# A hybrid decoder step: V, keys and keys' Gram of the recurrence on the opposite half of the array, and another order of VectorE's turn

## The chip, the cores and the metric

The kernel runs on one core of a Trainium2 chip. The metric is device time in microseconds of one execution: before the change the median of three runs is 1163.49 us (1162.94 to 1168.54).

## The reference, cut to what matters

One inference step of a decoder layer for 1024 prompt rows and 8 x 8 sample rows: a combined input projection, a convolution group and an RWKV-7 group side by side, an output projection, and a mixture of experts. The change touches the RWKV-7 recurrence alone, which runs for 8 heads of 64 channels:

```
def wkv_step(S, inp):
    r_t, w_t, k_t, v_t, kk_t, a_t = inp
    sa = einsum('bhvk,bhk->bhv', S, -kk_t)
    S = (S * w_t[:, :, None, :] + sa[..., None] * (kk_t * a_t)[:, :, None, :]
         + v_t[..., None] * k_t[:, :, None, :])
    y = einsum('bhvk,bhk->bhv', S, r_t)
    return S, y
```

Around it stand the token shift, the decay and the in-context learning rate from small projections, a norm of the keys per head, a group norm of y, a bonus term and an output gate.

## The kernel before, in words

The recurrence is computed in chunks of 64 tokens. Two chunks, 128 tokens, are one turn: turns j = 0 to 7 are the prompt, turn 8 the 64 sample rows. Two heads share the 128 partitions (channels p = 0 to 63 and 64 to 127), and there are four such pairs (CT = 4, index hp). Nearly every product of the recurrence is thus eight 64 x 64 matmuls, four on the array tile with rows and columns 0 to 63, four on the tile with rows and columns 64 to 127, taken in turn (`heads`, L1647).

Each engine has its own written-out program, in order, and they meet by semaphores. In turn j, with i = j - 1:

- TensorE (loop at L1791) forms the Gram of the b keys of turn j (`gram`, L1665: products within a chunk of all tokens' keys with all scaled a and r), the decay and learning rate of turn j + 1, the tokens of V (`to_tokens`, L1656: a transpose by a matmul with the identity), then for turn i the first product of level 4 (`level_y`), the first chunk's right-hand side (`chain_rhs`), the rest of level 4 (`level_x`), tokens of B, the Gram of the k keys of turn j, level 5's first product, tokens of K, the key norms of turn j + 1, the rest of level 5, y of turn i - 2 to channels, and then the chain for each of the two chunks: U (`chain_u`), the new state (`chain_s`), y (`chain_y`), the next right-hand side; between them bonus, cumulation of the decay for turn j + 1, and the gate of turn j - 3.
- Levels 4 and 5 combine inverses of 16 x 16 blocks to the inverse of a unit triangular 64 x 64 matrix. The inverses of the small blocks are made by VectorE on 64 partitions, one block each: SP moves the diagonal blocks to `u_blocks` in DRAM and back (L584, L587), VectorE works on `small_blocks` (L2425) and `whole_blocks` (L2434), ACT turns the result (`blocks_turned`, L1054), SP moves it by `x_blocks` (L592, L597) into XX, and TensorE's level 4 of the next turn waits for it (`inv_in`).
- VectorE (loop at L2513): masks the b Gram (`first_level`, L2394), adds the decay (`decay_add`, L2264), masks level 4 (L2416), the rest of the b Gram (L2402), centres the group norm, applies the conv norm, masks the k Gram (`masked_k`, L2408), masks level 5, small blocks, whole blocks, first new state (`new_state`, L2453 and L2456), keys (L2271, L2276), bonus (L2502), conv swish (L2477), scaled products (`scaled_a_b`, L2285 and L2290), gate (L2509), second new state, group norm's variance (L2492).
- ACT (loop at L1257) in a turn, in this order: root of the variance, the decay's tanh (L1035, L1037), copies of V, learning rate (L1068), right-hand side of the first chunk (L1186), level 4 (L1178), B, wide norms (L1051), conv tanh (L1228, L1232), copies of K, level 5 (L1182), U (L1191), group norm's affine (L1217), **the turned blocks (L1056)**, y of the first chunk (L1197), the second right-hand side (L1186), the three exponentials for turn j + 1 (L1095 to L1097), U of the second chunk (L1191), the square, the key scale (L1044), y of the second chunk.
- GpSimd multiplies scaled r and k (L827, L832, L839) and parts of the group norm.

TensorE's next turn begins with a wait for the scaled products (`prod_done`), the exponentials need the cumulation of the decay, and a new state must be there (`s_done`) before the next right-hand side. The first right-hand side of a turn stands between level 4's first product and its second, which needs VectorE's mask of the first. The last turn is followed by the samples' own stage (L1880 on), which uses the same V, keys and Gram tiles.

## Time and profile before

| | |
|---|---|
| median of three runs | 1163.49 us |
| profiled execution | 1164.35 us |
| its span | 1162.6 us |
| PE busy in the span | 1101.3 us |
| DVE busy | 672.4 us |
| ACT busy | 364.5 us |
| GpSimd busy | 223.9 us |

The recurrence's turns lie between about 364 and 600 us of the span. A timeline row gives the start, the time from the first start to the last end of a merged run of equal instructions, the line, the operation, how many there are, and in brackets how long the engine was idle before them and what ended that. Matmuls overlap, so a group's next neighbour starts before its last end. A windows row gives for a stretch each engine's busy time with its instruction count, TensorE's granted clock (1.00 is 2.4 GHz, 0.50 is 1.2 GHz), and the DMA share.

### The profile page before, as it was taken

The page shows a single profiled execution, that of the slowest core. Times are in us where ns is not written, and L with a number is a line of the kernel's source. Part 1 is how long each engine was busy: PE and PEld are TensorE (multiplying, and loading weights), DVE is VectorE, ACT ScalarE, POOL GpSimd, SP SyncE. Part 2 cuts the span into 40 slices and gives each one's busy share as a digit, 9 for nine tenths or more (in the row PEclk, how much of TensorE's full clock was granted, in tenths as well). Part 3 has the DMA queues.
Part 4 walks back from the last instruction along what each step waited for, and adds up shares of the span by engine and source line. Part 5 has one row for each costly group of instructions (what it writes and reads, how often), then busy time and mean ns, then how long its engine had stood idle before and what let it go on. Part 6 is the DMA issues. An engine that isn't in the chain of part 4 may idle for free.

```text
span 1162.6 us, 24205 instructions
## 1 busy us (share of the span) xinstructions
PE 1101.3 (95%) x9388; PEld 667.2 (57%) x9389; DVE 672.4 (58%) x1143; ACT 364.5 (31%) x720; POOL 223.9 (19%) x278
## 2 busy tenths in 40 slices
PE   6999999999999799999999999976999999999987
PEld 4666666666666688999994555444333333333342
DVE  6188999992554688888843332456334343433417
ACT  6000001111322657777651221022133223232324
POOL 6000000010002212332320001001223333342110
PEclk9999999999999899999999999977999999999999
DMA  9211111110000111111132421148898889999839
GB/s 289 71 35 35 34 33 36 43 43 23 1 1 5 16 17 22 19 19 19 38 120 98 136 73 37 46 176 332 343 367 324 312 318 344 413 413 402 335 111 401
DMA packets 97292, 171.42 MB, mean 147 GB/s; under 512 B 44377, under 2 KB 68624, under 8 KB 87921
## 3 DMA queue, kind: packets, MB, share of 16 engines
q1 hardware_dynamic: 89713, 152.31, 36.8%
q0 software_dynamic: 7488, 17.84, 4.4%
q8 instruction: 65, 1.06, 0.4%
q14 instruction: 26, 0.21, 0.1%
HBM read 153.63 MB, written 25.91 MB: 154 GB/s over the span
## 4 chain that ended last, share of the span: by engine, by line
PE 82%; DVE 8%; DMA 5%; ACT 2%; issue 2%; SPq 1%; POOLq 0%; ACTq 0%; DVEq 0%
PE ps L1640 27%; PE ps L2105 14%; PE ps L1955 10%; PE ps L2135 8%; PE ps L1652 5%; PE ps L1673 2%; PE ps L2092 2%; PE ps L2170 1%; DVE arena L2442 1%; PE ps L1985 1%; PE ps L1661 1%; DMA arena<-in_w_exp_down_dram 1%; DVE arena L2445 1%; DMA arena<-y_rows 1%; PE ps L2121 1%
## 5 line engine op out<-in xcount | busy, mean ns | idle before, releaser
L1640 PE MATMUL ps<-arena 128*128 128x384 f32 (+1 forms) x1040 | 319.2, 468 | 0.0
L1640 PEld LDWEIGHTS ps<-arena 128*128 128x128 f32 x1040 | 196.9, 190 | 119.1 <-issue 1.9
L2105 PE MATMUL ps<-arena 128*64 x416 | 188.5, 596 | 3.2 <-DVE arena L2838 2.0
L2108 PE MATMUL ps<-arena 128*64 128x512 f32 x416 | 188.5, 596 | 0.0
L2256 DVE SCALAR_TENSOR_TENSOR arena<-arena,cw 128x1024 f32<-128x1024 f32 x240 | 168.2, 777 | 0.4
L2105 PEld LDWEIGHTS ps<-arena 128*64 128x64 f32 x416 | 54.5, 136 | 111.6 <-issue 111.5
L1955 PE MATMUL ps<-arena 128*128 128x512 f32 x256 | 113.1, 596 | 0.0
L1652 PE MATMUL ps<-arena 64*64 64x64 f32 x2960 | 98.5, 219 | 6.3 <-DVE arena L2456 2.0
L2135 PE MATMUL ps<-arena 128*64 x208 | 96.5, 607 | 2.4 <-ACT arena L1408 2.4
L1652 PEld LDWEIGHTS ps<-arena 64*64 64x64 f32 x2960 | 92.5, 135 | 9.1 <-issue 4.6
L2138 PE MATMUL ps<-arena 128*64 128x512 f32 x208 | 96.5, 607 | 0.0
L1955 PEld LDWEIGHTS ps<-arena 128*128 128x128 f32 x256 | 47.5, 190 | 57.1 <-issue 57.0
L849 POOL COPY lastz<-arena 128x1 f32<-128x1 f32 x14 | 11.4, 815 | 313.6 <-ACT arena L1124 313.6
L1118 ACT ACTIVATE arena<-ps 128x768 f32<-128x768 f32 x14 | 11.4, 812 | 185.9 <-PE ps L1640 185.9
L943 POOL DMA_INDIRECT late<-xn_rows,g_idx x24 | 64.0, 2665 | 20.4 <-POOL g_idx L940 20.4
L2859 DVE COPY arena<-arena 128x4096 f32 x26 | 59.4, 2283 | 8.4 <-issue 7.9
L2844 DVE TENSOR_TENSOR small<-ps,small 128x256 f32<-128x256 f32 x26 | 11.0, 424 | 89.6 <-ACT small L1392 89.6
L2135 PEld LDWEIGHTS ps<-arena 128*64 128x64 f32 x208 | 26.8, 138 | 53.1 <-issue 53.1
L2868 DVE COPY arena<-ps 128x256 f32<-128x256 f32 x26 | 11.0, 424 | 77.4 <-PE ps L2121 77.4
L2108 PEld LDWEIGHTS ps<-arena 128*64 128x64 f32 x416 | 54.5, 136 | 0.0
L1408 ACT ACTIVATE arena<-arena 128x2048 f32 x26 | 49.6, 1908 | 13.9 <-SPq L690 12.6
L1392 ACT ACTIVATE small<-ps 128x256 f32<-128x256 f32 x26 | 10.0, 383 | 116.5 <-PE ps L2108 116.5
(362 smaller groups left out, 1537.3 us busy)
## 6 DMA issues: line engine op xcount, KB each, us to landing
arena<-in_w_exp_gate_dram SPq DMA_DIRECT2D x32, 1024.0 KB
arena<-in_w_exp_up_dram SPq DMA_DIRECT2D x32, 1024.0 KB
arena<-in_w_exp_down_dram SPq DMA_DIRECT2D x32, 1024.0 KB, 10.4
arena<-in_w_in_dram SPq DMA_DIRECT2D x22, 512.0 KB, 4.1
arena<-in_x_prompt_dram SPq DMA_DIRECT2D x16, 512.0 KB, 8.1
arena<-y_rows SPq DMA_DIRECT2D x8, 1024.0 KB, 16.7
arena<-in_w_out_dram SPq DMA_DIRECT2D x2, 2048.0 KB, 10.7
xn_rows<-arena SPq DMA_DIRECT2D x8, 512.0 KB, 2.8
```

What stands on the lines that cost most here:

```text
L943: pool.indirect_dma_start(out=xg[b], out_offset=None, in_=xn2_rows, in_offset=bass.IndirectOffsetOnAxis(ap=g_idx[b][:, :], axis=0), bounds ...
L1408: act.activation(wd.rearrange("p c n -> p (c n)"), wring[:, bass.ds(slot, 1), 2 * DC * F:].rearrange("p a n -> p (a n)"), ACT.Copy)\
L1640: ins = pe.matmul(banks(proj_bank(q) + piece)[:, 0:n1 - n0], win[q % 6][:, c, :], xnT[:, c, n0:n1], start=(c == 0), stop=(c == DC - 1))
L1652: ins = pe.matmul(dst[h, hp * 64:hp * 64 + 64], lhs[h, hp, :], rhs[h, hp, :], start=alone or (first and hp == 0), stop=alone or last, skip ...
L1673: ins = pe.matmul(banks(2 + c)[h, hp * P:(hp + 1) * P], lhs[h, hp, t], AR[j % 3][h, hp, :, t], start=True, stop=True)
L1955: ins = pe.matmul(banks(2 * (i % 2) + half)[0:r, :], lhs, wout[c // CT][:, c % CT, half * 512:half * 512 + 512], start=(c == 0), stop=(c = ...
L2105: pe.matmul(banks(b)[0:HS, :], xgT[b][:, c, 0:HS], wring_gu[:, bass.ds(slot, 1), 0:2, c, :].rearrange("p a w f -> p (a w) f"), start=(c == ...
L2108: ins = pe.matmul(banks(b)[HS:P, :], xgT[b][:, c, HS:P], wgu[b][:, :, c, :], start=(c == 0), stop=(c == DC - 1))
L2135: pe.matmul(banks(5 + half)[0:HS, :], hT[:, c, 0:HS], wring[:, bass.ds(slot, 1), n0:n0 + 512].rearrange("p a n -> p (a n)"), start=(c == 0 ...
L2138: ins = pe.matmul(banks(5 + half)[HS:P, :], hT[:, c, HS:P], wd[:, c, half * 512:half * 512 + 512], start=(c == 0), stop=(c == 1))
L2256: dve.scalar_tensor_tensor(out=dst, in0=src, scalar=w, in1=dst, op0=ALU.mult, op1=ALU.add).then_inc(conv_tap, 1)
L2859: dve.tensor_copy(wgu[b].rearrange("p w c f -> p (w c f)"), wring[:, bass.ds(slot, 1), 0:2 * DC * F].rearrange("p a n -> p (a n)"))\
```

## The change

Keys, V and what comes of the Gram of the k keys are kept on the opposite half of the partitions: a head whose channels are on partitions 0 to 63 has its tokens of V, tokens of K and its k Gram on 64 to 127, and the other way round. The products that make them, and those that use them, then run on the two array tiles off the diagonal (rows 0 to 63 with columns 64 to 127, and the reverse). In TensorE's program they are interleaved, matmul by matmul, with a group on the diagonal tiles:

- V's tokens with level 4's first product; K's tokens with level 5's; B's tokens (diagonal) with the k Gram;
- the first chunk's right-hand side, k Gram times V, with half of level 4's rest; this right-hand side moves behind level 4's first product and its mask;
- k Gram times V of y with U; keys times V of the new state with r times the old state of y.

Where a sum in one PSUM region is begun by matmuls off the diagonal and continued on it, TensorE waits for its own earlier matmuls by a new semaphore, `across_done`. The samples' stage gets six such waits. VectorE's turn is reordered. ACT's, GpSimd's and SP's programs are unchanged. The core of the diff:

```diff
+            def head_across(dst, lhs, rhs, hp, p, first=True, last=True):
+                o = other(p)
+                return pe.matmul(dst[p:p + 64, hp * 64:hp * 64 + 64], lhs[o, hp, :], rhs[o, hp, :],
+                                 start=first and hp == 0, stop=last, skip_group_check=True)
+            def turn_head(dst, src, c, hp, p, across):
+                h = slice(p, p + 64)
+                return pe.matmul(dst[other(p) if across else h, (c * CT + hp) * 64:(c * CT + hp + 1) * 64],
+                                 src[h, hp, c * 64:c * 64 + 64], ident[h, h], start=True, stop=True)
...
+            def gram_k_and_b_tokens(j):
+                pe.wait_ge(prod2_done, j + 1)
+                pe.wait_ge(gb_done, j + 1)
+                if j:
+                    pe.wait_ge(decay_sum, min(j + 2, NT))
+                for c in range(chunks_of(j)):
+                    for hp in range(CT):
+                        for p in (0, 64):
+                            g = gram_head(j, kt, c, hp, p, True)
+                            if j:
+                                ins = turn_head(banks(1), bt, c, hp, p, False)
...
+            def level_x4_and_rhs(i):
+                rhs_ready(i, 0)
+                pe.wait_ge(mm_done, level_count(i, 4, 0))
+                xt = XX[:, 1, 0, :, :]
+                for hp in range(CT):
+                    for p in (0, 64):
+                        ins = head_across(banks(7)[:, 0:256], GK[i % 2][:, 0, :, 0, :], vtok[i % 2][:, 0, :, :], hp, p,
+                                          last=False)
+                        head(banks(4)[:, 0:256], xt, MM[:, 0, :, :], hp, p, alone=True)
+                mark(ins)
+                heads(banks(4)[:, 256:512], MM[:, 0, :, :], xt, alone=True).then_inc(xx_psum, 1)
+                rhs_from_state(i, 0)
...
+            def chain_s_and_y(i, c):
+                n = 2 * i + c
+                t = slice(c * 64, c * 64 + 64)
+                state, y = banks(7)[:, 0:256], banks(2 + c)[:, 0:256]
+                pe.wait_ge(u_done, n + 1)
+                pe.wait_ge(across_done, crossed[0])
+                for hp in range(CT):
+                    for p in (0, 64):
+                        ins = head_across(state, ktok[i % 2][:, c, :, :], vtok[i % 2][:, c, :, :], hp, p, last=False)
+                        head(y, AR[i % 3][:, :, 1, t], SS[n % 2], hp, p, first=False, last=False)
+                mark(ins)
+                pe.wait_ge(across_done, crossed[0])
+                heads(state, btok[i % 2][:, c, :, :], UU, first=False).then_inc(s_psum, 1)
+                heads(y, GB1[i % 2][:, c, :, :], UU, first=False).then_inc(y_psum, 1)
...
                 if j:
                     level_masks(j - 1, 5)
+                keys(j + 1)
                 small_blocks(j)
-                whole_blocks(j)
                 if j:
                     new_state(j - 1, 0)
-                keys(j + 1)
+                whole_blocks(j)
+                scaled_a_b(j + 1)
                 if j:
+                    new_state(j - 1, 1)
                     bonus_v(j - 1)
                     conv_swish(j - 1)
-                scaled_a_b(j + 1)
                 if j >= 3:
                     gated(j - 3, 4)
-                if j:
-                    new_state(j - 1, 1)
                 if j >= 2:
                     gn_variance(j - 2)
```

## Rows read from the trace of the kernel before

**Rows 1.** The page: busy us, share of the span, instructions of each engine.

```profile
PE 1101.3 (95%) x9388; PEld 667.2 (57%) x9389; DVE 672.4 (58%) x1143; ACT 364.5 (31%) x720; POOL 223.9 (19%) x278
```

**Rows 2.** Windows: stretch, length, busy us of PE, PEld, DVE, ACT, POOL, clock, DMA.

```profile
402.20:557.70 155.50, 149.02 (x3850) 140.65 (x3847) 131.21 (x266) 109.21 (x247) 47.53 (x39) 1.00 0.12 18
494.28:504.15 9.87, 9.87 (x276) 9.58 (x273) 8.92 (x15) 8.26 (x18) 4.19 (x4) 1.00 0.14 16
498.97:509.45 10.48, 10.48 (x318) 10.24 (x314) 8.08 (x22) 8.98 (x22) 2.72 (x2) 1.00 0.10 16
```

**Rows 3.** One line's instructions, L2408: min, median, max ns, first and last start.

```profile
L2408 DVE TENSOR_TENSOR arena<-ps,small x9: 692/1224/1226, 379.0 to 582.3; 128x1024 f32<-128x1024 f32 x8, 128x512 f32<-128x512 f32 x1
```

**Rows 4.** Timeline of PE in one turn: start us, us, line, what, count.

```profile
496.80 0.69 PE L1522 MATMUL ps<-late,arena 64*128 64x512 f32 x1
496.81 0.71 PE L1528 MATMUL ps<-arena 64*128 64x128 f32 x4
...
502.61 1.10 PE L1661 MATMUL ps<-ident,arena 64*64 64x64 f32 x32
503.54 1.92 PE L1673 MATMUL ps<-arena 64*64 64x128 f32 x32
...
509.75 0.63 PE L1652 MATMUL ps<-arena 64*64 64x64 f32 x16
...
511.40 0.68 PE L1652 MATMUL ps<-arena,gain 64*64 64x64 f32 x16
```

**Rows 5.** The page's costliest groups: two tiles of the experts' matmuls.

```profile
L2105 PE MATMUL ps<-arena 128*64 x416 | 188.5, 596 | 3.2 <-DVE arena L2838 2.0
L2108 PE MATMUL ps<-arena 128*64 128x512 f32 x416 | 188.5, 596 | 0.0
```

**Rows 6.** Timeline of DVE in the same turn and just before it.

```profile
494.73 1.45 DVE L2456 TENSOR_TENSOR arena<-arena 128x256 f32<-128x256 f32 x1
...
499.55 0.89 DVE L2416 TENSOR_TENSOR arena<-ps,mask_lv 128x256 f32<-128x256 f32 x2 [0.62 <-PE ps L1652]
...
505.50 1.23 DVE L2408 TENSOR_TENSOR arena<-ps,small 128x1024 f32<-128x1024 f32 x1 [1.36 <-PE ps L1673]
...
509.76 1.03 DVE L2442 TENSOR_TENSOR arena<-arena 64x512 f32<-64x512 f32 x1
...
513.21 0.41 DVE L2453 TENSOR_TENSOR arena<-ps,arena 128x256 f32<-128x256 f32 x1
513.65 0.43 DVE L2456 TENSOR_TENSOR arena<-arena 128x256 f32<-128x256 f32 x1
...
516.42 0.68 DVE L2477 SCALAR_TENSOR_TENSOR arena<-arena 128x512 f32<-128x512 f32 x1
517.59 1.32 DVE L2285 SCALAR_TENSOR_TENSOR arena<-arena 128x512 f32<-128x512 f32 x1 [0.48 <-issue]
...
520.47 1.45 DVE L2456 TENSOR_TENSOR arena<-arena 128x256 f32<-128x256 f32 x1
```

**Rows 7.** Timeline of ACT in the same turn.

```profile
498.97 0.63 ACT L1035 ACTIVATE arena<-arena 128x512 f32<-128x512 f32 x1 [0.50 <-DVE arena L2264]
...
513.32 0.64 ACT L1056 ACTIVATE arena<-arena 64x256 f32<-64x256 f32 x1 [1.10 <-DVE arena L2445]
...
516.41 0.60 ACT L1095 ACTIVATE arena<-ps 128x512 f32<-128x512 f32 x1 [0.71 <-PE ps L1611]
...
517.86 0.41 ACT L1191 ACTIVATE arena<-ps 128x256 f32<-128x256 f32 x1
```

**Rows 8.** Timeline of SP's queue: DMA issues to and from x_blocks.

```profile
513.99 1.62 SPq L592 DMA_DIRECT2D x_blocks<-arena  x2
517.20 4.22 SPq L597 DMA_DIRECT2D arena<-x_blocks  x8
```

**Rows 9.** Windows: the clock at the start of the samples' stage.

```profile
601.50:604.70 3.20, 3.03 (x57) 3.06 (x59) 3.05 (x7) 1.28 (x4) 0.00 (x0) 0.50 0.58 147
```

**Rows 10.** Timeline of PE there.

```profile
601.67 0.58 PE L1652 MATMUL ps<-arena 64*64 64x64 f32 x6 [1.64 <-DVE arena L2584]
```

More of the change, by code:

```diff
@@ L397, in hybrid_decoder_step @@
         tok_psum, tok_done = sem("tok_psum"), sem("tok_done")
+        across_done = sem("across_done")
         gb_psum, gk_psum, gb_done, gk_done, pt_done = (sem(n) for n in (
@@ L1645, in _, with other, head @@
                 between(q - NCONV)
+            def other(p):
+                return slice(64 - p, 128 - p)
+            def head(dst, lhs, rhs, hp, p, first=True, last=True, alone=False):
+                h = slice(p, p + 64)
+                return pe.matmul(dst[h, hp * 64:hp * 64 + 64], lhs[h, hp, :], rhs[h, hp, :],
+                                 start=alone or (first and hp == 0), stop=alone or last, skip_group_check=True)
+            def head_across(dst, lhs, rhs, hp, p, first=True, last=True):
+                o = other(p)
+                return pe.matmul(dst[p:p + 64, hp * 64:hp * 64 + 64], lhs[o, hp, :], rhs[o, hp, :],
+                                 start=first and hp == 0, stop=last, skip_group_check=True)
             def heads(dst, lhs, rhs, first=True, last=True, alone=False):
@@ L1889, in _ @@
             q8 = i8 % 2
-            heads(banks(2)[:, 0:256], GK[q8][:, 0, :, 0, :], vtok[q8][:, 0, :, :], last=False)
+            mark(heads_across(banks(2)[:, 0:256], GK[q8][:, 0, :, 0, :], vtok[q8][:, 0, :, :], last=False))
+            pe.wait_ge(across_done, crossed[0])
             for hp in range(CT):
```

154 lines of the change are left out of this document (86 added, 68 removed).

## The prediction, made before the change was run

> **What bounds the kernel now.** I read the page first: TensorE is busy 95% of the span [rows 1], so a stall or extra matmul time in the recurrence shows. Then the windows: from 402.2 to 557.7 us (six turns of the recurrence) TensorE is busy 149.0 of 155.5 us at full clock, DVE 131.2, ACT 109.2 [rows 2]. So PE sets the pace, but DVE has only 4 us of room in a turn: PE cannot be made much faster before DVE, ACT or a chain between them takes over. I call M the start of the masked keys' Gram on DVE (L2408). Its nine starts from 379.0 to 582.3 us give eight intervals of 25.4 us on average [rows 3].
>
> **PE's own time.** 32 small matmuls start between 502.61 and 503.54 us: 16 pairs in 0.93 us, 58 ns for a pair on the two diagonal tiles of the array; the 32 of a Gram take 1.92 less the last one's tail, 1.75 us [rows 4]. The change puts matmuls on the other two tiles between these pairs. What it can hide in a full turn: V beside level 4's first product, B's tokens beside the keys' Gram, K's tokens beside level 5's: 32 matmuls each, 3 x 0.93 = 2.8 us; keys' Gram times V beside level 4 (first right-hand side) and beside the two U, keys times V beside the state's part of the two y: 16 each, 5 x 0.47 = 2.3 us. Together 5.1 us, if four tiles run side by side. The rows say that they do: tiles with the same rows and different columns (L2105 and L2108) start 832 matmuls in 189 us of union, 227 ns each where one lasts 596 [rows 5]; tiles with the same columns and different rows (L1522, L1528) start 10 ns apart, and the one's 0.69 us holds four of the other's [rows 4]. I take full overlap.
>
> The weight loads of L2108 run beside L2105's matmul on the same 128 rows, else the pair could not cost 2 x 227 ns [rows 5]. The Trainium skill, TensorE: Matmul & The Clock Gate, Part 3 (Packing small matmuls), states the opposite: a weight load overlaps matmuls in flight only when the row group differs. By that rule the four-tile groups would serialise and nothing would be hidden, which is the last rival below. The row decides against it here.
>
> What it adds on PE is waits for its own matmuls (across_done). No row shows PE waiting for itself. Low bound: the last matmul's tail, 0.17 us (one lasts 0.22: 16 take 0.63 at 509.75, seven steps of 0.058 off). High bound: a whole matmul, and a hand-over such as that from PE to DVE at M, 0.04 to 0.1 (503.54 + 1.92 to 505.50): 0.32 us [rows 4, 6]. I take 0.23. The one in the first right-hand side lies behind 16 matmuls and costs nothing; three a turn (second right-hand side, both new states) are exposed: 0.7 us. Queued behind each is the group that ends the sum for which ACT or DVE waits. Net on PE: 5.1 - 0.7 = 4.4 us less per turn. Were that all, PE would need 21.3 us a turn, and DVE's 22 would be the bound.
>
> **DVE's reordering, and what stands behind it.** In the turn I follow M is at 505.50, and a plain full turn is 25.75 us long (the same L2456 at 494.73 and 520.47) [rows 6]. Before, DVE goes from M over masks and small blocks straight to the whole blocks (L2442 from 509.76, M + 4.3), done when L2453 starts at 513.21 (M + 7.7) [rows 6]. ACT turns them at 513.32 (L1056) [rows 7], and SP issues the DMAs to x_blocks from 513.99 on and back from 517.20 [rows 8]. The change puts the keys (514.07 to 515.8, just ahead of bonus and swish: 1.75 us) before the small blocks, and the first new state before the whole blocks. So the small blocks end at M + 6.05, and then DVE waits for the first state's sum from PE. When is that there?
>
> - ACT's work from the decay's tanh to the copies of level 5 is nearly solid: 8.98 busy of 10.48 us (498.97 to 509.45) [rows 2]. DVE's decay sum (L2264) releases its start, at M - 6.5 before [rows 7]. In the new turn DVE has no hole from there to M (499.55 to M less its last hole, 4.6 us of masks, Gram mask and norms), so ACT starts at M - 4.6 and ends level 5's copies at M + 4.4.
> - Then PE: from U's matmuls to the state's, 509.75 to 511.40, 1.65 us [rows 4]: M + 6.1. New state: 0.47 (four tiles), self-wait 0.23, 0.47, tail and hand-over 0.25: **M + 7.6**, against M + 7.0 before (511.40 + 0.93 + 0.17). So a wait of 1.5 us appears on DVE.
> - New state 0.87 (513.21 to 514.08), whole blocks 3.5 (509.76 to 513.21): they end at **M + 12.0** instead of M + 7.7 [rows 6].
>
> ACT executes in order, and its order is not changed: turning the blocks still stands ahead of the copies of y and of the second right-hand side, of the three exponentials and of U's copy. All wait for M + 12.0: turned 0.7, y 0.3, right-hand side 0.3, exponentials 1.45 (516.41 to 517.86), U 0.4 [rows 7]: M + 15.3. PE then needs 0.5 + 0.23 + 0.47 + 0.25 for the second state: M + 16.75. DVE's scaled products need the second exponential, M + 14.5, a hole of 2.5 us, and end at 16.4, just in the shade of that. From the second state's sum to the next M, DVE has solid work: 8.9 us busy in 494.28 to 504.15 [rows 2] (second state with its L2456 of 1.45 us, first Gram's mask, decay, level 4's masks, norms) and bonus, swish and gate, 3 x 0.6 (as 516.42) [rows 6]: 10.7. **Next M = 16.75 + 10.7 = 27.5.**
>
> A second loop goes by DMA: blocks turned at M + 12.7; from 513.99 the last issue back ends at 517.20 + 4.22 and lands some 1.4 us later, 8.8 us [rows 8]. So level 4 starts at M + 21.5; its mask is there 1.1 us later; 0.47 x 3 + 0.93 for level 4 and right-hand side, 1.75 the Gram, 0.25 hand-over: M' = 27.0. (The right-hand side, which covered that mask, now stands behind it.)
>
> So a full turn goes from 25.75 to 27.5 us although PE has 4.4 us less to do. The L2456 of 1.45 us is 0.43 at 513.65, and L2285 takes 1.32 where a like operation takes 0.68 (516.42) [rows 6]; what stretches them no row here shows. If the first is short in its new place, the second loop rules, 27.0.
>
> **The sum.** Eight intervals: the first +0.6 (inverse 1.8 later by the keys ahead of it, 1.2 recovered between level 4 and M), two with no group norm yet at 27.0, +1.3 each, four at 27.5, +1.8 each, the last +1.5: 11.9. Stage of the samples: six self-waits, 1.5, less about 0.8 hidden in the last turn: +0.7. Together +12.6 us. The profiled execution took 1164.35 us with a span of 1162.6; the median of the runs is 1163.49, 0.9 below. From the median: **1176 us** (1.1% slower). Its own range is 1170 to 1183 (0.5 us per turn either way, self-waits at either bound).
>
> **Rivals.**
> - *The clock falls in the new holes.* PE is through at about M + 10.7 and would idle 2.7 us before the second U, and 1.7 before level 4. For it: from 601.5 to 604.7 the clock was at 0.50, 1.2 GHz [rows 9], after an idle of 1.64 us before 601.67 [rows 10]. Against: in the six turns, with their short holes, it stays at 1.00 [rows 2]. A half-clock stretch of 3.2 us over U, gate and second state costs about 1.3 us on the path; in most of seven turns, +9: 1185. Chance 0.14.
> - *The first state comes early, and the saving arrives (faster).* The turn is the time of the state's sum after M, plus 0.87 + 3.5 + 4.75 + 10.7 = 19.8. ACT has 1.5 us of holes ahead of U and PE gets 4.4. Were the sum there at M + 4.5, the turn would be 24.3, eight of them -11.5 us: 1152. It decides at M + 5.9; ACT's solid 9 us before U speak against it. Chance 0.08.
> - *No change.* The same sum at about M + 6.05, when the small blocks end: 25.9 a turn, 1163 to 1168. Chance 0.08.
> - *Four tiles do not overlap.* Then 4.2 us come back onto the path (three groups of 0.93 and three of 0.47): 31.7 a turn, +45: about 1208. Against it stand rows 4 and 5. Chance 0.03.
>
> My forecast has 0.67. About 0.5% (5.8 us) is what a measurement tells from no change. Faster 0.08; same 0.09 (the third rival and the forecast's own edge); slower 0.83. The range takes in the clock's rival and the upper edge of no change: 1168 to 1190.
>
> **What would show it.** In the profile after: M to M about 27 to 27.5 us; DVE idle over 1 us before the first new state, and over 2 us before the scaled products, released by ACT's exponential; ACT idle 4 to 5 us before it turns the blocks; PE idle over 2 us before the second U, and before level 4, released by the DMA from x_blocks; a four-tile group of 64 matmuls in about 0.95 us. Wrong: whole blocks ending before M + 10, M to M under 25.7, or mixed groups taking twice 0.93 us.

## The result, and the profile after

The changed kernel took **1190.36 us** (median of 4 runs, 1190.03 to 1191.15), the kernel before 1165.19 us beside it (4 runs, 1162.94 to 1168.54): a ratio of 1.0205, with a 95% interval of 1.018 to 1.0229. It is slower, as forecast, but by 25 us where I had put 12.6; 1190.36 also lies just outside the range. Of the 14.4 us between the forecast of 1176 and 1190.36, 1.7 lie in the kernel before, which took 1163.49 when I forecast and 1165.19 beside this one.

The page after, busy time of each engine, answers to [rows 1]:

```profile
PE 1088.7 (92%) x9388; PEld 645.7 (54%) x9389; DVE 671.2 (56%) x1143; ACT 359.7 (30%) x720; POOL 221.5 (19%) x278
```

The same instructions, and TensorE has 12.6 us less to do. The windows after, the six turns that answer to the first of [rows 2] and then three single turns:

```profile
404.47:575.23 170.76, 136.60 (x3859) 123.68 (x3853) 128.73 (x266) 105.09 (x246) 48.40 (x39) 0.92 0.11 17
432.81:460.57 27.76, 22.05 (x629) 20.04 (x624) 21.49 (x44) 17.11 (x39) 6.45 (x6) 0.88 0.11 18
489.82:518.31 28.49, 22.92 (x666) 20.64 (x659) 21.63 (x45) 18.50 (x43) 8.02 (x7) 0.94 0.10 14
518.31:546.66 28.35, 23.17 (x670) 20.90 (x666) 21.61 (x45) 18.50 (x43) 8.51 (x8) 0.94 0.11 18
```

Six turns took 155.5 us and take 170.8. PE is idle for 34 us of them (6.5 before), and the granted clock is no longer 1.00: each turn has one stretch at 0.50, of 3.4 us or of twice that. The masked keys' Gram on DVE, the line whose starts are M, answers to [rows 3]:

```profile
L2489 DVE TENSOR_TENSOR arena<-ps,small x9: 693/1223/1226, 378.3 to 603.2; 128x1024 f32<-128x1024 f32 x8, 128x512 f32<-128x512 f32 x1
```

| M to M, us | 1st | 2nd | 3rd | 4th | 5th | 6th | 7th | 8th |
|---|---|---|---|---|---|---|---|---|
| before | 23.22 | 25.75 | 25.73 | 25.75 | 26.06 | 25.75 | 26.53 | 24.50 |
| after | 26.20 | 28.34 | 27.77 | 29.25 | 28.49 | 28.35 | 28.57 | 27.93 |

The profiled executions differ by 26.0 us of span (1162.6 and 1188.6): 21.6 in these eight intervals, 3.4 between the last M and the first projection (36.6 before, 40.0 after), -0.7 ahead of the first M and 1.7 behind the projection's start. I take the turn from M = 518.31. DVE after, which answers to [rows 6]:

```profile
526.07 0.42 DVE L2534 TENSOR_TENSOR arena<-ps,arena 128x256 f32<-128x256 f32 x1 [1.54 <-PE ps L1653]
...
529.69 0.68 DVE L2526 TENSOR_REDUCE arena<-arena 64x64 f32<-64x512 f32 x1
...
532.62 1.32 DVE L2366 SCALAR_TENSOR_TENSOR arena<-arena 128x512 f32<-128x512 f32 x1 [2.25 <-ACT arena L1097]
...
536.24 0.42 DVE L2534 TENSOR_TENSOR arena<-ps,arena 128x256 f32<-128x256 f32 x1 [1.70 <-PE ps L1653]
536.70 0.42 DVE L2537 TENSOR_TENSOR arena<-arena 128x256 f32<-128x256 f32 x1
```

First state at M + 7.76 after 1.54 us of waiting (forecast 7.6 and 1.5), whole blocks done at M + 12.06 (12.0), scaled products at M + 14.31 after 2.25 (14.5 and 2.5): DVE's chain is as forecast up to there. The second state is not: M + 17.93, forecast 16.75. ACT and SP after, which answer to [rows 7] and [rows 8]:

```profile
530.40 0.63 ACT L1057 ACTIVATE arena<-arena 64x256 f32<-64x256 f32 x1 [5.09 <-DVE arena L2526]
```

```profile
531.05 1.20 SPq L593 DMA_DIRECT2D x_blocks<-arena  x2
533.89 4.40 SPq L598 DMA_DIRECT2D arena<-x_blocks  x8
```

ACT has its idle time of 5.09 us ahead of the turned blocks (forecast 4 to 5), and the issues back run to M + 20.0. PE after: the start of level 4 with V's tokens, which answers to [rows 4], and the second U with what follows it:

```profile
512.00 0.24 PE L1653 MATMUL ps<-arena 64*64 64x64 f32 x1 [0.97 <-DMA arena<-x_blocks]
512.00 0.27 PE L1675 MATMUL ps<-ident,arena 64*64 64x64 f32 x1
...
512.93 0.22 PE L1653 MATMUL ps<-arena 64*64 64x64 f32 x1
512.94 0.22 PE L1675 MATMUL ps<-ident,arena 64*64 64x64 f32 x1
...
531.62 0.37 PE L1653 MATMUL ps<-arena 64*64 64x64 f32 x1 [2.08 <-ACT arena L1187]
...
532.68 2.07 PE L1838 MATMUL ps<-arena,late 128*128 128x128 f32 x8
```

The 64 matmuls on four tiles start within 0.94 us, as 32 on two tiles did [rows 4]: four tiles run side by side (forecast 0.95). But the hole of 2.08 us ahead of the second U is followed by U with starts 0.1 us apart per group of four, and by eight matmuls of the gate in 2.07 us; the window over them gives the clock:

```profile
531.40:534.80 3.40, 3.19 (x44) 2.85 (x48) 1.92 (x2) 3.40 (x9) 1.87 (x2) 0.51 0.14 39
```

That is the level of 1.2 GHz, half of 2.4, as in [rows 9], here after an idle time of 2.08 us as there after 1.64 [rows 10]. In the seven turns from M = 404.47 on, such a stretch occurs each time: in five over U and the gate (second state then at M + 17.4 to 18.0), in two (from M = 460.57 and 546.66) over level 4 and the Gram (second state at M + 16.5, and M', the next M, late). In these two the same 2.08 us of idle time stand ahead of the second U, and the clock stays at 1.00 behind them; it falls behind the idle time ahead of level 4, 2.67 and 1.22 us. What ended the waits of the six turns, in order of total time (us, times, longest):

```profile
DVE arena L2534 <- PE ps L1653: 15.7, 12, 1.7
...
DVE arena L2366 <- ACT arena L1097: 13.5, 6, 2.3
PE ps L1653 <- ACT arena L1187: 12.5, 6, 2.1
...
PE ps L1653 <- DMA arena<-x_blocks: 5.2, 4, 2.7
```

### The profile page after: what moved, and what is told of

The parts are those of the page before. It is cut to its first block, busy times and chain, and to the rows that moved or that the text cites. A ratio compares the mean times of both kernels' runs of the same rounds, so it can differ in the third digit from the quotient of the medians.

```text
span 1188.6 us, 24232 instructions
## 1 busy us (share of the span) xinstructions
PE 1088.7 (92%) x9388; PEld 645.7 (54%) x9389; DVE 671.2 (56%) x1143; ACT 359.7 (30%) x720; POOL 221.5 (19%) x278
## 4 chain that ended last, share of the span: by engine, by line
PE 82%; DVE 7%; DMA 4%; issue 3%; ACT 2%; SPq 2%; POOLq 0%; DVEq 0%; ACTq 0%
PE ps L1641 27%; PE ps L2186 15%; PE ps L2036 9%; PE ps L2216 8%; PE ps L1653 5%; PE ps L2173 2%; PE ps L1688 2%; PE ps L2251 2%; PE ps L1658 1%; PE ps L2066 1%; DVE arena L2523 1%; SPq L598 1%; DVE arena L2526 1%; PE ps L1675 1%; DMA arena<-in_w_exp_up_dram 1%
## 5 line engine op out<-in xcount | busy, mean ns | idle before, releaser
L1653 PEld LDWEIGHTS ps<-arena 64*64 64x64 f32 x2416 | 89.5, 148 | 41.5 <-issue 16.5
L1409 ACT ACTIVATE arena<-arena 128x2048 f32 x26 | 49.6, 1908 | 15.8 <-SPq L691 14.7
L1688 PE MATMUL ps<-arena 64*64 64x128 f32 x544 | 39.9, 301 | 7.6 <-DVE arena L2371 7.6
## 6 DMA issues: line engine op xcount, KB each, us to landing
arena<-in_w_exp_down_dram SPq DMA_DIRECT2D x32, 1024.0 KB, 10.4
```

The costliest lines, as they stand in the source:

```text
L1409: act.activation(wd.rearrange("p c n -> p (c n)"), wring[:, bass.ds(slot, 1), 2 * DC * F:].rearrange("p a n -> p (a n)"), ACT.Copy)\
L1653: return pe.matmul(dst[h, hp * 64:hp * 64 + 64], lhs[h, hp, :], rhs[h, hp, :], start=alone or (first and hp == 0), stop=alone or last, ski ...
L1688: return pe.matmul(banks(2 + c)[other(p) if across else h, hp * P:(hp + 1) * P], lhs[h, hp, t], AR[j % 3][h, hp, :, t], start=True, stop=True)
```

## The experiments

My theory behind them: the new order sets the path, and two things lie on top of what I summed up. The loop through x_blocks is longer than I took it, and the clock is halved in the new holes. Rivals: either alone; the self-waits; the halves.

**1. The halves alone** (DVE's old order put back):

```
                 masked_k(j, mask_ar)
                 if j:
                     level_masks(j - 1, 5)
-                keys(j + 1)
                 small_blocks(j)
+                whole_blocks(j)
                 if j:
                     new_state(j - 1, 0)
-                whole_blocks(j)
-                scaled_a_b(j + 1)
+                keys(j + 1)
                 if j:
-                    new_state(j - 1, 1)
                     bonus_v(j - 1)
                     conv_swish(j - 1)
+                scaled_a_b(j + 1)
...
+                if j:
+                    new_state(j - 1, 1)
```

> The changed kernel with VectorE's old order (small blocks, whole blocks, first new state, keys, bonus, swish, scaled products, gate, second new state); the products on the opposite half stay. Theory (the order costs, the halves gain): whole blocks end again at about M + 7.8, PE needs some 21.3 us a turn, DVE and ACT become the bound: M to M 24.5 to 25.2 us instead of 28.4, the clock stays at 1.00 in full turns, time 1156 to 1161 us, faster than before. Rival (the halves cost: four-tile groups or the waits of PE for itself are dear): M to M above 25.75, time 1166 us or more. A middle result, 1161 to 1166, would say that the hidden matmuls are given back at once as waits for DVE and ACT.

Measured: 1174.88 us (10 runs), ratio 1.0074 (1.0047 to 1.0101). My expectation failed by its sign. Turns of 25.3 and 25.4 us come first, then 27.6 to 29.9. In the turn from M = 505.90 DVE and then PE show why:

```profile
510.86 0.16 DVE L2511 TENSOR_TENSOR arena<-arena 64x12 f32<-64x12 f32 x1 [3.07 <-DMA arena<-u_blocks]
...
517.70 0.41 DVE L2534 TENSOR_TENSOR arena<-ps,arena 128x256 f32<-128x256 f32 x1
518.14 0.43 DVE L2537 TENSOR_TENSOR arena<-arena 128x256 f32<-128x256 f32 x1
```

```profile
518.62 1.12 PE L1658 MATMUL ps<-arena 64*64 64x64 f32 x16 [4.61 <-DVE arena L2537]
```

With a shorter turn the other DMA chain (u_blocks, out and in again) is not back when DVE wants the blocks (M + 2.7 to 4.9 in those turns). In the turn shown the state behind the blocks comes at M + 11.8, PE idles 4.6 us, and the clock halves there as well. That is what the saved 4.4 us of PE meet.

**2. The order alone** (the kernel before, with the same lines of DVE moved the other way):

> The kernel before with VectorE's new order alone; no product changes its half. Theory (the order costs): the first new state's wait on DVE and the turned blocks late on ACT appear as in the changed kernel, M to M 27.5 to 28.5 us, time 1178 to 1187 us. Rival (the order is harmless without the new PE program, since PE sets the pace): M to M 25.7 to 26.2, time 1163 to 1168 us.

Measured: 1189.76 us (4 runs), ratio 1.0201 (1.0147 to 1.0255), somewhat above the theory. So the order alone is enough for the slowdown (+23 us); the halves alone cost +8, and both together +25. That the two don't add up to 31 would fit a gain of PE's that covers a part of what the order costs, but 6 us are no more than the intervals of the three ratios leave open: it is not shown. Turns 27.9 to 30.0; ACT's wait ahead of the turned blocks in the turn from M = 432.60:

```profile
443.97 0.63 ACT L1056 ACTIVATE arena<-arena 64x256 f32<-64x256 f32 x1 [6.21 <-DVE arena L2445]
```

**3. The self-waits alone** (the kernel before, with PE waiting for its last matmul at the three places of each turn):

```
+            def own(ins):
+                owned[0] += 1
+                ins.then_inc(own_done, 1)
+                pe.wait_ge(own_done, owned[0])
...
-                heads(banks(7)[:, 0:256], ktok[i % 2][:, c, :, :], vtok[i % 2][:, c, :, :], last=False)
+                own(heads(banks(7)[:, 0:256], ktok[i % 2][:, c, :, :], vtok[i % 2][:, c, :, :], last=False))
```

> The kernel before with three waits of PE for its own matmuls in each of turns 1 to 8 (after the first group of the second right-hand side and of both new states), nothing else. It prices the wait where PE sets the pace. Theory (0.23 us each, all on the path): 24 waits, +5.6 us, M to M 26.4 instead of 25.75, time 1168 to 1172 us. Rival (the waits are hidden or shorter): within 2 us of before. Rival (dear, 0.5 us each): 1178 us and more.

Measured: 1169.18 us (10 runs), ratio 1.0034 (1.0019 to 1.0049); a plain turn takes 26.3 instead of 25.75, 0.18 us for each wait. The term was right (I had taken 0.23).

**4, 5 and 6. The hole filled.** Identity matmuls into a free bank ahead of the second U, 18 of them, then 9, then 9 and another 5 ahead of level 4:

```
+                if 0 < j < NT - 1:
+                    for n in range(9):
+                        pe.matmul(banks(4)[:, 0:P], ident[:, :], ident[:, :], start=True, stop=True)
```

> The changed kernel with 18 matmuls of the identity by itself (128 x 128, into a bank that the gate overwrites) put into PE's hole of 2.3 us before the second U of turns 1 to 7; they compute nothing that is used. Theory (the clock halves after that hole and stretches U, gate and second state): granted clock 1.00 through most turns, second state's sum at M + 16.8 instead of M + 17.9, M to M 27.2 to 27.6 us, time 1181 to 1184 us. Rival (my chain was too short for another reason): the clock rises, but M to M stays at 28.2 or more and the time at 1188 to 1191 us.

> The changed kernel with 9 matmuls of the identity by itself in PE's hole before the second U of turns 1 to 7 (each is two passes in the trace, some 2.0 us in all; 18 took 4.0 us and overfilled the hole). They compute nothing that is used. Theory (the clock's halving stretches the path by about 1 us a turn): second state's sum at M + 16.5, clock at 1.00 in most turns, M to M 26.9 to 27.4 us, time 1178 to 1183 us. Rival (clock is not the cause): M to M stays above 28, time 1188 to 1192 us. If the halving only moves to the hole before level 4, the time is between.

> As the kernel with 9 matmuls in the hole before the second U, and 5 more (1.1 us) in the hole before level 4 in turns 2 to 8. Theory: clock at 1.00 throughout turns 2 to 7, M to M 26.9 to 27.3 us, time 1177 to 1182 us, no slower than with the first hole alone. Rival: M to M above 28.

Measured: 1201.24 us (ratio 1.028, 1.0245 to 1.0316), 1191.4 (1.0247, 1.0205 to 1.0289) and 1190.8 (1.021, 1.0177 to 1.0242). The first was overfilled: each of its matmuls stands as two in the trace, so 18 take 4.0 us where the hole has 2. The second and third fill the holes without overfilling the first. The kernel with nine, in five turns and in one of them:

```profile
433.69:572.92 139.23, 118.27 (x3335) 107.11 (x3329) 108.54 (x224) 91.47 (x211) 42.48 (x34) 0.99 0.11 18
```

```profile
534.70 0.42 DVE L2537 TENSOR_TENSOR arena<-ps,arena 128x256 f32<-128x256 f32 x1 [0.34 <-PE ps L1653]
540.89 0.89 DVE L2500 TENSOR_TENSOR arena<-ps,mask_lv 128x256 f32<-128x256 f32 x2 [0.52 <-PE ps L1653]
545.74 1.23 DVE L2492 TENSOR_TENSOR arena<-ps,small 128x1024 f32<-128x1024 f32 x1 [0.25 <-PE ps L1688]
```

The clock is back at 0.99, and the second state comes at M + 16.57 (M is 518.13), as forecast. Yet DVE then waits for level 4, which waits for x_blocks, and the turns still take 27.9 us on average. In the kernel with both holes filled the clock is at 1.00 in all of the 2nd to 7th intervals, and they too average 27.9. So the theory that the clock alone is the surplus falls. The median did not move (1191.4 for 1190.4). In the profiled execution, which is the fastest of its four, the six intervals gave back 3.1 us, but the first became longer by 1.5 and the last by 0.6.

**7. ACT's turned blocks behind the second copy of U:**

> The changed kernel with ACT's turning of the blocks moved behind its copy of the second U (turns 1 to 7), so that y's copy, the second right-hand side, the exponentials and U no longer wait for the whole blocks. Theory (two loops, ACT's order holds one of them): DVE's hole of 2.25 us before the scaled products and PE's before the second U go, but the blocks are turned some 0.7 us later and the loop by DMA rules: M to M 27.5 to 28, level 4 waits over 2 us for the DMA from x_blocks, time 1183 to 1188 us. Rival (there is only the loop by DVE): M to M 24.7 to 25.5, time 1160 to 1166 us. Rival (ACT's order is not what holds): no change, 1189 to 1191 us.

Measured: 1194.05 us (4 runs), ratio 1.0228 (1.0198 to 1.0257). The second state moved from M + 17.9 to M + 14.7, as it should, and nothing was won: the blocks were turned 0.9 us later, and PE's wait for the DMA grew. The waits of the same six turns:

```profile
PE ps L1653 <- DMA arena<-x_blocks: 15.8, 4, 5.3
```

**8. The halves alone, with six identity matmuls ahead of the second right-hand side:**

> VectorE's old order with the products on the opposite half, and 6 matmuls of the identity (1.3 us) in PE's hole before the second right-hand side of turns 1 to 7, where it waits for the first new state. Theory (in that kernel the wait for the small blocks' DMA makes a hole of up to 4.7 us, the clock halves after it): M to M 25.3 to 26.3 instead of 27.6 to 29.9 in turns 3 to 7, time 1160 to 1168 us. Rival (the waits for DMA and GpSimd's overlap with the whole blocks set it, not the clock): 1172 to 1178 us, with the clock at 1.00.

Measured: 1171.46 us (7 runs), ratio 1.005 (1.0034 to 1.0066). Where the clock held, the turns took 24.8 to 25.7 us: five of them, 25.2 on average, where the same five took 26.0 before the change. That is what the halves gave here of the 4.4 us, 0.7 a turn. But one took 30.2 (u_blocks back at M + 4.95), and the last M to the projection took 42.6 with a half-clock stretch of 17 us in it.

**9 and 10. The way back from x_blocks on two queues.** Four of the eight DMAs are issued by ACT, ahead of its key scaling; then the same with nine matmuls in the hole:

```
+                if 0 < j < NT - 1:
+                    blocks_back(j)      # waits for x_blocks, issues DMAs 4 to 7 from ACT
                 if j < NT - 1:
                     key_scale(j + 1)
                 if j:
                     y_copy(i, 1, 3)
```

> The changed kernel, with the eight DMAs that bring x_blocks back (4.4 us of issues on SP alone) issued four by SP and four by ACT, ahead of its key scaling, in turns 1 to 7. Output is the reference's. In the changed kernel a full turn is M to M 28.3 us on average, and the way from the turned blocks to the landing is 9.6 us, with another 5.8 to 6.7 us to the next M. Theory (the loop through the DMAs rules, at 27.3 to 27.7, and the clock adds up to it): the way falls by about 2.2 us to 7.4, the last landing is at M + 19.5, TensorE no longer waits for x_blocks ahead of level 4, and the other loop, DVE's, takes over: second state at M + 16.5 and 10.4 us of solid DVE behind it, 26.9, and up to 27.8 where the clock is halved over the second U. So intervals of 27.3 on average, 1 us less in seven turns: 1184 us (1181 to 1187). Rival (the half clock alone makes the time): intervals stay at 28.0 to 28.5 and the time at 1188 to 1192, with level 4 released by DVE's first Gram mask instead of the DMA. Rival (ACT's 2.2 us of issues delay what stands behind them): key scaling ends 2.2 us later, GpSimd's keys too, and the time is not lower though the landing is.

> The same, and beside it the nine identity matmuls (about 2 us) ahead of the second U in turns 1 to 7, which by themselves kept the clock at 1.00 in most turns and changed nothing in the time (1191.4). Theory: with the DMA loop shortened and the clock held both surplus terms are gone and the plain DVE loop is left: second state at M + 16.5, plus 10.4: intervals of 27.0 (26.8 to 27.2), 1.3 us less than in the changed kernel in each of seven turns: 1181 us (1178 to 1184). If the loop by DMA is not what held the filled kernel at 28.0, its intervals stay there and the time at 1190.

Measured: 1191.26 us (ratio 1.0204, 1.0169 to 1.0239) and 1196.9 (1.0229, 1.019 to 1.0267). The last landing moved from M + 21.3 to 22.2 up to M + 19.2 to 21.1, and the time did not follow: the third case that I had named. The turn from M = 460.70 is at full clock, and DVE in it:

```profile
477.22 0.42 DVE L2545 TENSOR_TENSOR arena<-ps,arena 128x256 f32<-128x256 f32 x1 [0.29 <-PE ps L1664]
...
481.30 0.69 DVE L2486 TENSOR_TENSOR arena<-ps,small 128x512 f32<-128x512 f32 x1 [0.80 <-PE ps L1699]
```

After the second state, 0.80 us are lost to the Gram of B, which waits for ACT's second copy of y, and that now stands behind ACT's four issues. My edit put a wait of its own in the place of the one removed, so these two don't decide.

**11 and 12. No way back.** The DMAs back are left out in turns 1 to 7, and level 4 uses turn 0's blocks, so the values of the recurrence are others (and perhaps the routing): the turns are to be read, not the whole time. Without and with nine matmuls in the hole:

```
                 if j:
-                    sp.wait_ge(inv_in, 16 * 2 * NB * j)
+                    sp.wait_ge(inv_in, 16 * 2 * NB)
...
                 sp.wait_ge(inv_out, 32 * (j + 1))
                 if j:
-                    sp.wait_ge(xx_psum, level_count(j - 1, 4, 1))
+                    return
...
-                        pe.wait_ge(inv_in, 16 * 2 * NB * (i + 1))
+                        pe.wait_ge(inv_in, 16 * 2 * NB)
```

> The changed kernel without the DMAs that bring the blocks back in turns 1 to 7: the inverse's level 4 uses those of turn 0 in every turn (the recurrence's values are wrong by that, and the routing of tokens behind it may differ, so the intervals M to M are to be read, not the whole time). Nothing waits for x_blocks any more and no other engine issues anything in its place, as ACT did in the kernel with the split. Theory (two loops, DVE's at 26.9 and the one by DMA at 27.3 to 27.7, and a halved stretch adds about 0.9 to the first): intervals of 26.9 in turns in which the second state's sum is there at M + 16.5, 27.8 where the clock is halved over it; 27.3 on average against 28.4. Rival (the clock alone): 28 and more as before, each turn with its halved stretch.

> The same in the kernel with nine identity matmuls ahead of the second U. Both surplus terms are gone, so only DVE's own loop is left: the second state's sum at M + 16.5 and 10.4 us of solid DVE: 26.9 in each turn (26.8 to 27.1), against 28.0 with the matmuls alone. If they stay near 28.0, neither the DMAs nor the clock make the difference and DVE's work behind the second state is longer than I read.

Measured: 1183.7 us (2 runs, ratio 1.0171, 1.0128 to 1.0214) and 1182.12 (2 runs, 1.0157, 1.0107 to 1.0207). The windows of single turns without the matmuls, three at full clock and one with a halved stretch, then those of the kernel with them:

```profile
459.85:486.80 26.95, 21.38 (x649) 19.25 (x641) 21.63 (x45) 18.48 (x43) 8.90 (x8) 1.00 0.07 13
515.57:542.52 26.95, 21.76 (x670) 19.65 (x666) 21.64 (x46) 18.48 (x43) 8.60 (x8) 1.00 0.07 14
542.52:569.47 26.95, 22.09 (x669) 19.54 (x664) 21.64 (x45) 18.22 (x43) 8.90 (x8) 1.00 0.06 13
486.80:515.57 28.77, 23.28 (x678) 20.87 (x678) 21.64 (x46) 18.52 (x43) 8.94 (x8) 0.94 0.06 12
```

```profile
485.89:513.76 27.87, 23.51 (x687) 21.45 (x682) 22.69 (x46) 18.53 (x43) 8.96 (x8) 1.00 0.06 12
513.76:540.86 27.10, 23.82 (x687) 21.62 (x682) 21.64 (x45) 18.52 (x43) 8.93 (x8) 1.00 0.06 13
540.86:567.85 26.99, 24.23 (x687) 21.63 (x682) 21.64 (x46) 18.26 (x43) 8.94 (x8) 1.00 0.07 14
```

26.95 three times over is DVE's loop by itself: the second state's sum at M + 16.5 and 10.4 us of work. The hole ahead of the second U is still there in these three turns, and the clock stays at 1.00 behind it; in the turn from M = 515.57:

```profile
528.88 0.27 PE L1653 MATMUL ps<-arena 64*64 64x64 f32 x1 [2.09 <-ACT arena L1187]
```

The turn of 27.87 waits for the other DMA chain, and so does the one of 27.83 before it: u_blocks lands at M + 5.2 and 5.1 there, DVE waits for it, and the first state starts at M + 8.6 instead of 7.8. In the turn from M = 485.89:

```profile
491.11 0.17 DVE L2514 TENSOR_TENSOR arena<-arena 64x12 f32<-64x12 f32 x1 [1.32 <-DMA arena<-u_blocks]
```

The average of the 2nd to 7th interval in the four kernels:

| | DMAs back | none back |
|---|---|---|
| holes as they are | 28.46 | 27.64 |
| nine matmuls in the hole | 27.94 | 27.19 |

The DMA loop is worth 0.8 us a turn, the clock 0.5, both 1.3. Neither does it alone. Each average is that of one profiled execution, and the clock differs in a part of the turns only: without the DMAs and the matmuls three of the six intervals have a halved stretch (27.8 to 28.8 us) and three have none (26.95); with the matmuls and the DMAs two have one (28.4 and 28.9) and four have none (27.2 to 28.0, 27.6 on average). So a halved stretch goes with 1.0 to 1.4 us more in the turn that has it, and at full clock the DMA loop is worth 0.6.

**13 and 14. The remaining terms taken away.** ACT's copies and exponentials ahead of the turned blocks: first with ACT's four DMAs where they stood, then behind the copy of y.

```
-                elif j:
-                    blocks_turned(j)
-                else:
+                elif j == 0:
                     exps(1)
                     blocks_turned(0)
...
                 if 0 < j < NT - 1:
                     exps(j + 1)
+                    blocks_turned(j)
                 if j:
                     u_copy(2 * i + 1)
```

> The split of the DMAs back, and beside it ACT's order: copy of y, copy of the second right-hand side and the three exponentials stand ahead of the turning of the blocks, which stands ahead of the copy of U. What ACT did after its 5 us of waiting it now does in that wait. Theory: the exponentials are done by about M + 11, the blocks are turned at M + 12.1 as before, U's copy at M + 12.8, PE hands over the second state's sum at M + 14.6, DVE's scaled products start without a wait at M + 12.1 and the second state at M + 14.6: DVE loop 14.6 + 10.4 = 25.0 to 25.4; loop by DMA 12.1 + 0.6 + 7.4 + 5.8 = 25.3 to 25.9. So intervals of about 25.5, the first interval and the stage of the samples as in the changed kernel (2.4 to 3 and 3.4 us longer than before): 1169 us (1166 to 1173), no change against the kernel before. Rival (halved clock in whatever hole is left ahead of level 4): one halved stretch a turn, 26.5, 1177.

> As the kernel with ACT's new order (copies and exponentials ahead of the turning of the blocks), whose intervals of 30 us came from my place for ACT's four DMAs: they stood ahead of the key scaling and of the second copy of y, waited 2.7 us for x_blocks, and the Gram of B, which waits for that copy, came 4 us late. Here they stand behind both. Theory: copy of y at M + 15.5, ACT's four issues from M + 16.1 to 18.1, landing at M + 19.6; level 4 no longer waits for it; second state at M + 15.2 as measured there, and 10.4 us behind it: intervals of 25.6 (25.2 to 26.0), 1168 us (1165 to 1173). Rival (another hole ahead of level 4 halves the clock again): 26.5, 1176.

Measured: 1203.79 us (ratio 1.0306, 1.0275 to 1.0338), then 1178.75 (1.0134, 1.0076 to 1.0191). In the first the copy of y stood behind ACT's wait for x_blocks at M + 19.5, and DVE waited 3.6 us for the Gram of B. In the second three turns took 25.62, 25.62 and 25.61 us: the 25.6 that I had expected. The turn from M = 508.46, on DVE:

```profile
520.92 1.31 DVE L2376 SCALAR_TENSOR_TENSOR arena<-arena 128x512 f32<-128x512 f32 x1 [0.40 <-ACT arena L1106]
...
523.65 0.42 DVE L2544 TENSOR_TENSOR arena<-ps,arena 128x256 f32<-128x256 f32 x1 [0.82 <-PE ps L1663]
...
534.09 1.22 DVE L2499 TENSOR_TENSOR arena<-ps,small 128x1024 f32<-128x1024 f32 x1 [0.30 <-PE ps L1698]
```

The wait of 2.25 us is 0.40, and the second state stands at M + 15.19. The earlier turns took 26.2 to 26.4 and the last 28.8 with a halved stretch; that is 5.4 us of the more than 10 by which the whole lies above the 1168 that I had expected.

**15. Turn 0's keys behind its blocks again:**

> The same, with the keys behind the whole blocks in turn 0 as before the change (there is no state to compute yet, so the new order has nothing to hide behind them). Theory: the first interval falls from 26.2 back to 23.3, and the time by that, 2.8 us, against the kernel with ACT's order alone: 1165 to 1166 us. If the inverse's DMAs are not what waits in turn 0, nothing changes.

Measured: 1175.82 us (5 runs), ratio 1.012 (1.0086 to 1.0155). The first interval fell from 26.14 to 22.05 us, more than the 2.8 expected, but two later turns with a halved stretch took 27.3 and 27.2. The second of them, and the turn behind it at full clock:

```profile
479.49:506.71 27.22, 22.73 (x669) 20.83 (x664) 21.82 (x45) 18.93 (x43) 8.99 (x8) 0.94 0.12 18
506.71:532.41 25.70, 21.47 (x667) 19.35 (x663) 21.70 (x45) 18.73 (x43) 8.21 (x8) 1.00 0.12 19
```

Against the kernel of 14 the gain of 3 us is smaller than the spread of its own runs.

**16 and 17. The samples' turn on its own half**, in the changed kernel and in the kernel of 15:

```
-                            g = gram_head(j, kt, c, hp, p, True)
+                            g = gram_head(j, kt, c, hp, p, j < NT - 1)
...
-                                v = turn_head(banks(0), src, c, hp, p, True)
+                                v = turn_head(banks(0), src, c, hp, p, j < NT - 1)
```

> The changed kernel, with V, K's tokens and the keys' Gram of the last turn (the samples') on their own half as before the change, so that the stage of the samples has no matmul across halves and none of its six self-waits. Turns 1 to 7 are the changed kernel's. From the start of the last masked Gram to the first projection took 36.6 us before, 40.0 in the changed kernel, 35.0 with DVE's new order alone and 40.5 with the halves alone, so the surplus of 3.4 us goes with the halves. Theory (the self-waits in new_states and the right-hand sides, 1.5 us, and the clock that their holes halve): with them gone the stretch is 36 to 37.5 us and the time 3 us less, 1187. Rival (turn 7's part of that stretch and the clock inherited from the holes ahead of it make it): 39 to 40, and the time does not move.

> The version that the experiments point to: halves in turns 0 to 7, ACT's copies and exponentials ahead of the turned blocks, four of the eight DMAs back issued by ACT behind the copy of y, the keys behind the blocks in turn 0, and the samples' turn on its own half. The kernel without the last of these took 1175.8 us (span 1167.0), with full turns of 25.7 to 27.3 us and 40.2 us from the last masked Gram to the projection. Theory: that stretch falls to 37, the first interval is 22 and the full turns 26.3 on average: span 1163, and 1166 to 1172 in the median, no measured change against the kernel before. Rival (as the one above): 1175.

Measured: 1188.79 us (4 runs), ratio 1.0204 (1.0175 to 1.0234), and 1173.44 (6 runs), ratio 1.0079 (1.0057 to 1.01). The stretch from the last M to the projection is 40.0 us in the first, unchanged: the theory (self-waits in the samples' stage) is wrong. In the other it fell from 40.2 to 38.3, but that is not shown to be the samples' doing: turn 7's first state stands at M + 9.7 there and at M + 11.1 in the kernel of 15, and at M + 9.7 in the kernel of experiment 1 as well, which keeps the samples on the other half. This best version is still 0.8% slower than the kernel before.

## Why the prediction was right and wrong, by its steps

The profiled executions differ by 26.0 us where 12.6 were forecast. The 13.4 us more lie in the 2nd to 7th interval (5.4), the first (2.4), the last (1.9), the stretch from the last M to the projection (2.7), and outside of all these (1.0 net).

- **PE's own time: right.** Four tiles side by side (0.94 us for 64 matmuls), self-waits at 0.18 us (experiment 3), PE 2.1 us a turn less busy even with halved stretches. The rule of the Trainium skill, TensorE: Matmul & The Clock Gate, Part 3 (Packing small matmuls), by which a weight load overlaps matmuls in flight only when the row group differs, is contradicted by the trace after, as it was by [rows 5]: the 0.94 us hold pairs of tiles with the same rows.
- **DVE's chain up to the scaled products: right**, each stamp within 0.2 us. The DVE loop that follows from it, forecast at 27.5, is 26.95 in undisturbed turns: the second state's sum is there at M + 16.5 and not 16.75 (ACT's terms as I gave them add up to M + 15.15, where I wrote 15.3), and 10.4 us of work follow and not 10.7. Its second instruction took 0.42 us in its new place in five of the seven turns, and not 1.45, the case that I had left open (what stretches it stands in the last section).
- **The failed step: "a second loop ... by DMA: ... M' = 27.0"**, put below DVE's 27.5 and so left out of the four turns' term. The way from the turned blocks (M + 12.7) to the landing was nearly right: 8.6 to 9.5 us in the seven turns, 9.0 on average, for 8.8. From the landing to M' I took 5.5, all at full clock and with DVE waiting ready: it is 5.7 to 6.0 us at best and 6.5 to 7.1 in most turns. So this loop is 27.5 us undisturbed, above DVE's own 26.95 and not below it. Its price by the table: 0.8 us a turn, 4.8 in six turns. What makes the way from the landing to M' longer than my 5.5 even at full clock, no run took apart.
- **The other failed step: the clock, put at nothing in the sum and given 0.14 as a rival. It came true in every turn.** I had argued from the short holes of before. Its price where it lies over U was right (second state 0.9 to 1.45 us later, 1.3 forecast), but a part is hidden by the DMA loop, so it is worth 0.5 a turn by the table. Where it lies over level 4 and the Gram, it lengthens the DMA loop itself. The forecast and this rival were not alternatives: the holes that the forecast itself described are where the clock fell. They did not do so each time, though. Ahead of the second U the same 2.1 us of idle time were followed by half clock in nine of 14 turns (five of seven in the changed kernel, four of seven in the one without the way back) and by full clock in the other five.
- **The sum of the turns.** For the 2nd to 7th interval I forecast 9.8 us more, which is 27.56 a turn; with both surplus terms taken away it is 27.19, so what I summed is too long by 0.4, not too short. The 1.3 us of the two terms come on top: 28.46, or 15.2 us more in six turns. The last interval is 3.4 us longer and not 1.5.
- **The first interval: +3.0, not +0.6.** Experiment 15 splits it. With the old order it is 22.05, 1.17 under before: the 1.2 to be recovered are there. The keys ahead put the end of the whole blocks from M + 7.3 to 10.2, 2.8 us and not 1.8 (the keys took 2.1, and the small blocks 3.4 instead of 2.5), and from the landing to M' it took 6.9 and not 5.7, with a halved stretch at 398.3 us.
- **The samples' stage: +3.4, not +0.7.** The surplus goes with the halves and not with the order: with the order alone the stretch takes 35.0 us, with the halves alone 40.5. But it is not the samples' own products (experiment 16): the second state of turn 7 stands at 622.19, M + 19.0, where before it stood at 597.65, M + 15.4. All of the 3.4 us (and 0.3 more) have arisen by then: 1.95 by the first state, 1.7 between the two. In the first part PE idles where it did not before (1.06 us at 605), in the second it waits 0.99 us for DVE's L2537, which takes 1.54 us beside GpSimd (last section), and the gate runs at half clock behind it (2.07 us for 1.16). The windows from the last M to that second state, after and before:

```profile
603.16:622.19 19.03, 16.44 (x417) 14.59 (x408) 5.35 (x9) 11.07 (x26) 6.36 (x5) 0.91 0.08 12
```

```profile
582.29:597.65 15.36, 15.31 (x391) 14.42 (x388) 4.88 (x10) 9.90 (x23) 6.37 (x5) 1.00 0.19 30
```

What starts the hole at 605 is open; no run took it away.
- **The other rivals.** An early first state, and no change: the state's sum came at M + 7.7, neither. Experiments 13 and 14 show what the order would have needed: ACT's work ahead of the turned blocks and a shorter way back, then 25.6, no more than before. Of the 4.4 us that PE was freed of, the turns of experiment 8 had 0.7 at best; DVE has 21.6 us of work in a turn, and the two DMA chains hang on it.

Why the same kernel has turns of 25.6 and of 27 us can be read from the windows: in the kernels of 14, 15 and 17 the ten of the 4th to 7th intervals at full clock took 25.6 to 26.2 us, the two with a halved stretch 27.2 and 27.3. The landing of u_blocks tells them apart only where it is very late, at M + 5.1 or more; below that a turn of 25.6 has it at M + 3.8 and one of 27.2 at M + 0.7. What stays open: why the clock falls behind a hole in one turn and not behind the same hole in the next, why u_blocks is late at times, and the hole at 605.

## What to carry to other kernels

Before moving work on an engine that is nearly full, sum each loop that closes through its waits (here DVE with ACT and PE, and DVE with ACT, the DMAs and PE) to the end, and where two come within half a microsecond of each other, count on the longer one plus what varies from turn to turn. A hole of 2 us on TensorE that the change itself makes belongs into the forecast and not among its rivals: price what follows it at half clock, for a part of the turns, since here that came behind such a hole in nine turns of 14. Matmuls on free tiles are worth their time only where TensorE still sets the pace afterwards.

## What the runs showed of the hardware that I had not expected

- An identity matmul of 128x128 in f32 stands as two in the trace (in the kernel with nine, timeline of PE):

```profile
529.28 2.27 PE L1949 MATMUL ps<-ident 128*128 128x128 f32 x18
```

- The same idle time of 2.1 us ahead of the second U was followed by a clock of 0.50 in nine turns of 14 and by 1.00 in five. With both holes filled the clock stayed at 1.00 in six turns out of six that are otherwise the same (2nd to 7th interval); with the first alone filled, in four of six.
- Four DMAs of the same shape issued by ACT beside SP's four took 3.08 us in one turn and 1.87 in another; SP's four took 1.78 in both.
- The same DVE instruction of 128x256, the new state's second (L2456, L2537 after; both operands from the arena, none from PSUM), took 0.42, 1.05, 1.45 and 1.54 us in different places of a turn. By the traces it waits for a GpSimd instruction that is under way. Over all kernels here it took more than 0.47 us 76 times. Each time a TENSOR_TENSOR of GpSimd was running when it began, with at least 0.20 us to go, and each time it ended 0.28 us (0.278 to 0.287) behind the end of that one. In the other 228 cases it took 0.42 or 0.43, and GpSimd had at most 0.15 us to go or was not running. No run moved GpSimd's instruction by itself; the rule is read off the ends of all of them. The 1.45 us from 494.73 in [rows 6] stand over this one, which ends at 495.90:

```profile
494.63 1.27 POOL L832 TENSOR_TENSOR arena<-arena 128x512 f32<-128x512 f32 x1 [1.42 <-ACT arena L1044]
```
